# Router logits taken from residual rows that are not normalised, with the shift's part made ahead of the second attention

## The chip, the cores and the metric

The kernel runs on one core of a Trainium2 chip. The metric is the device time of one execution, in microseconds (us). A core has five engines that run their own instruction streams and meet at semaphores: TensorE (PE; its weight loads are PEld), VectorE (DVE), ScalarE (ACT), GpSimd (POOL) and SyncE (SP). SyncE here only issues transfers from the chip's memory.

## What is computed

A first block (a hybrid of two attentions) and a second block (attention over the rows and a context, then a mixture of experts with 16 experts) are applied to 256 rows of 1024 numbers. What matters here is the path from the second attention's output to the choice of rows for each expert:

```python
x = x + g_a * mix
h2 = modulate(rmsnorm(x, norm_ffn[l]), sh_f, sc_f)        # rmsnorm(...) * (1 + sc_f) + sh_f
x = x + g_f * ec_moe(h2, w_router[l], w_gate[l], w_up[l], w_down[l])
return rmsnorm(x, norm_final)

def ec_moe(h, w_router, w_gate, w_up, w_down):
    aff = jax.nn.softmax(jnp.einsum('bnd,de->bne', h, w_router, ...), axis=-1)
    vals, idx = lax.top_k(jnp.swapaxes(aff, 1, 2), cap)   # cap = 32 rows for each expert
    # each expert: gather its rows of h, silu(a) * u, down projection, scatter-add
```

All arithmetic that matters here is float32; a float32 matmul takes two passes of PE, and the profile counts each as one instruction.

## The kernel before, in words

**Tiling.** The 256 rows are two tiles `t` of 128 partitions, the 1024 columns two halves `h` of 512 or 8 chunks of 128. A name such as `ou01` or `rT10` is a group of work with a PSUM bank of its own turn: the two digits are tile and half. `DENSE` lists the groups ahead of the second attention, `TAIL` those behind it; every engine walks through the same lists in its own program. `BANK_OF` gives each group its bank; `filled` waits until PE has filled it, `leave` releases it and `kept` waits for that release.

**The tail.** Attention output `oT` is multiplied with the output weights: `first_output` makes `ou00` and `ou01` (tile 0, L1651), `tail` makes `ou10` and `ou11` (L1588). For each, DVE multiplies with the gate (L2333) and adds into the residual rows `xn`, which lie in `x_sb` (L2335), and ACT sums the squares (L770). Behind a tile's second half, `half_root` makes the mean (L1844), POOL the inverse root (L1092), and DVE scales both halves of the tile into `rn`, which lies in `rows` (L2340). PE then transposes (`rT..`, L1125), and ACT and DVE evacuate four chunks each into `uT`, with the factor `scl[:, 2, :]` and the shift `mc[:, 0, 24:32]` applied (`turned_mod`, L789 and L1859). `logits(t)` multiplies with `wr` in four column groups of the array (`lg`, L1568), DVE copies the four partial sums (L2306), `logit_sums(t)` adds them on PE (`ls`, L1576), and `softened(t)` with `soft(t)` makes the softmax. For tile 0 all this lies within the eight chunks of `ou11`: lg0 ahead of chunk 4, ls0 ahead of chunk 6. Then `afT` transposes the affinities, DVE searches the 32 largest of each expert (L2353), while PE puts `xn` into four banks (L1611, semaphore `x_added`), `slT` and `cuT` turn the choice into a one-hot matrix, `gx0` to `gx7` gather the chosen rows of `rn` and apply factor and shift, and the experts' products follow (L1717, L1763). `unread(n)` is n transposes that nobody reads; `WARM` says after which group how many of them stand.

**The stream of weights.** SyncE issues the slots of `STREAM` in order, each into a buffer that has to be free: slot OUT0's buffer is free when `ou10` is filled, OUT1's when `ou11` is. Each slot is 128 rows of 4096 numbers. The buffers in order, around the tail: `parts` (behind `ou10`), `parts` (behind `ou11`), then buffer 8 (pieces in `tz` and `lat`, 2048 numbers a row each), buffer 9 (3072 in `late_slot`, once `xn` is complete, and 1024 in `tz`, once lg1 is filled), then half of a slot into `x_sb` itself, once `x_added` is reached (L711), and then the ring again, its first half behind the first two expert products (`half_used`, L671). SyncE works in order: whatever waits in front holds back everything behind it. All expert weights together are 48 slots; 41 of them are issued from `ou11` on.

**Ahead of the second attention** PE makes, among others, qu00, qu01, xkv00 and xkv01 (L1136), while DVE applies rotations and waits.

## Time and profile before

| | |
|---|---|
| median of 3 runs | 659.83 us (658.94 to 660.0) |
| the profiled execution | 658.71 us, its span 656.9 us |
| PE busy | 588.6 us (90% of the span), mean granted clock 0.972 |
| PEld, DVE, ACT, POOL busy | 376.2, 286.7, 219.0, 41.9 us |
| transfers | 192.56 MB, mean 293 GB/s |
| chain that ended last | PE 66%, transfers 22%, DVE 5% |

The busy shares are means over stages with different limits. The page's 40 slices tell these apart: the DMA line is at 3 to 9 tenths with two holes up to slice 26, and at 9 tenths from slice 27 to the end, while the PE line falls from 9 to between 5 and 8 there. Each slice is 16.4 us, so slice 27 begins at 443 us, where the router stands.

### The profile page before, as it was taken

What the parts mean: (1) busy time and instruction counts of PE and PEld (TensorE: products, weight loads), DVE (VectorE), ACT (ScalarE), POOL (GpSimd) and SP (SyncE); (2) the same over time, 40 slices, a digit from 0 to 9 for tenths busy, and PEclk for the clock granted to TensorE, in tenths of its full rate; (3) what the DMA queues carried; (4) which work ended last, traced back from release to release, by engine and by line L of the source; (5) the groups of instructions that cost most, each with busy time, mean ns of one, the idle gap of its engine ahead of it and who ended that gap; (6) DMA issues with size and microseconds to landing.
All of it is one profiled execution on the core that took longest, in us unless ns stands there. A gap on an engine that the chain in (4) does not pass through costs nothing.

```text
span 656.9 us, 8818 instructions
## 1 busy us (share of the span) xinstructions
PE 588.6 (90%) x3513; PEld 376.2 (57%) x3513; DVE 286.7 (44%) x683; ACT 219.0 (33%) x477; POOL 41.9 (6%) x74
## 2 busy tenths in 40 slices
PE   6999999999999999999999999998989875667685
PEld 5988877778767787748755455455352421221232
DVE  3356577585658443566737867145220110010002
ACT  4345453554524423384426755121110100010002
POOL 3000000000000000110002443000000000000000
PEclk9999999999999999999999999999999887798899
DMA  8593866657697784675569003559999999999995
GB/s 355 178 392 144 347 256 232 261 215 285 257 376 278 279 343 142 245 261 199 212 256 356 29 1 129 219 186 409 402 429 430 428 426 426 428 421 432 428 418 214
DMA packets 19465, 192.56 MB, mean 293 GB/s; under 512 B 3552, under 2 KB 4960, under 8 KB 7136
## 3 DMA queue, kind: packets, MB, share of 16 engines
q1 hardware_dynamic: 15824, 188.49, 71.8%
q10 hardware_dynamic: 3312, 1.93, 1.0%
q0 software_dynamic: 288, 1.57, 0.6%
q8 instruction: 28, 0.46, 0.3%
q14 instruction: 13, 0.11, 0.1%
HBM read 190.41 MB, written 1.05 MB: 291 GB/s over the span
## 4 chain that ended last, share of the span: by engine, by line
PE 66%; DMA 22%; DVE 5%; ACT 2%; SPq 2%; issue 1%; POOL 0%; ACTq 0%; POOLq 0%; DVEq 0%
PE bank L1148 27%; DMA ring<-in_stream 21%; PE bank L1125 6%; PE bank L1136 5%; PE bank L1717 3%; PE bank L1422 3%; PE bank L1651 2%; PE bank L1187 2%; PE bank L1588 2%; PE bank L1556 2%; SPq L733 2%; PE bank L1523 2%; PE bank L1637 2%; PE bank L1479 2%; DMA vvc<-vvc 1%
## 5 line engine op out<-in xcount | busy, mean ns | idle before, releaser
L1148 PE MATMUL bank<-weight_parts,u_parts 128*128 128x512 f32 (+2 forms) x416 | 125.7, 385 | 0.7 <-DVE weight_parts L2027 0.5
L2027 DVE TENSOR_TENSOR weight_parts<-ring,weight_parts 128x1024 fp32r<-128x1024 f32 (+2 forms) x64 | 73.2, 1180 | 38.0 <-ACT weight_parts L759 36.2
L1148 PEld LDWEIGHTS bank<-weight_parts,u_parts 128*128 128x128 f32 x416 | 75.6, 188 | 18.0 <-issue 2.8
L759 ACT ACTIVATE weight_parts<-ring 128x1024 fp32r<-128x1024 f32 (+2 forms) x64 | 63.9, 1021 | 30.3 <-PE bank L1148 22.6
L1148 PE MATMUL bank<-weight_parts,x_parts 128*128 128x512 f32 (+1 forms) x128 | 48.4, 378 | 0.0
L1148 PE MATMUL bank<-u_parts,weight_parts 128*128 128x256 f32 x192 | 36.7, 288 | 0.7 <-DVE weight_parts L2027 0.6
L1092 POOL TENSOR_TENSOR small<-small 128x1 f32<-128x1 f32 (+1 forms) x14 | 8.3, 596 | 434.0 <-DVE small L2421 207.0
L823 ACT ACTIVATE sp<-sp,small 128x128 f32<-128x128 f32 (+1 forms) x48 | 21.3, 444 | 36.3 <-DVE small L1951 36.3
L1148 PEld LDWEIGHTS bank<-u_parts,weight_parts 128*128 128x128 f32 x192 | 30.5, 192 | 1.7 <-DVE weight_parts L2027 1.0
L1039 ACT ACTIVATE sp<-bank 128x512 f32<-128x512 f32 x4 | 2.4, 597 | 74.7 <-PE bank L1717 74.7
L1148 PE MATMUL bank<-x_parts,weight_parts 128*128 128x256 f32 x96 | 27.2, 283 | 0.0
L1717 PE MATMUL bank<-ring,tz 128*32 128x512 f32 x112 | 17.3, 747 | 10.8 <-DMA ring<-in_stream 10.8
L1148 PEld LDWEIGHTS bank<-weight_parts,x_parts 128*128 128x128 f32 x128 | 24.1, 188 | 4.5
L2395 DVE TENSOR_TENSOR sp<-sp,bank 128x512 f32<-128x512 f32 x4 | 2.8, 688 | 53.2 <-PE bank L1717 53.2
L2393 DVE SCALAR_TENSOR_TENSOR sp<-sp,bank 128x512 f32<-128x512 f32 x4 | 2.8, 688 | 51.2 <-ACT sp L1039 51.2
L1136 PE MATMUL bank<-ring,lat 128*128 128x512 f32 (+2 forms) x56 | 23.0, 555 | 0.4 <-ACT vvc L759 0.4
L1125 PE MATMUL bank<-ident 128*128 128x128 f32 x124 | 18.0, 291 | 4.8 <-DMA ident<-in_ident 4.8
L1125 PEld LDWEIGHTS bank<-ident 128*128 128x128 f32 x124 | 14.6, 150 | 13.4 <-issue 7.8
L1125 PE MATMUL bank<-ident,sp 128*128 128x128 f32 x152 | 21.2, 276 | 1.1 <-DVE sp L2014 0.8
L759 ACT ACTIVATE mo<-bank 128x512 f32<-128x512 f32 (+3 forms) x20 | 10.6, 541 | 33.0 <-PE bank L1148 16.6
L1125 PEld LDWEIGHTS bank<-ident,sp 128*128 128x128 f32 x152 | 17.4, 141 | 6.4 <-issue 3.3
L1008 ACT ACTIVATE tz<-bank,small 128x128 f32<-128x128 f32 x12 | 4.5, 456 | 42.5 <-PE bank L1637 42.5
(333 smaller groups left out, 1051.4 us busy)
## 6 DMA issues: line engine op xcount, KB each, us to landing
ring<-in_stream SPq DMA_DIRECT2D x41, 2048.0 KB, 8.9
parts<-in_stream SPq DMA_DIRECT2D x11, 2048.0 KB, 27.8
qk<-in_stream SPq DMA_DIRECT2D x9, 2048.0 KB, 12.2
tabs<-in_stream SPq DMA_DIRECT2D x6, 2048.0 KB, 20.4
mo<-in_stream SPq DMA_DIRECT2D x5, 2048.0 KB, 28.9
vvc<-in_stream SPq DMA_DIRECT2D x5, 2048.0 KB, 32.1
ring<-in_stream SPq DMA_DIRECT2D x5, 1024.0 KB, 31.0
tz<-in_stream SPq DMA_DIRECT2D x4, 1024.0 KB, 27.9
```

The source lines that it names most:

```text
L733: eng.dma_start(slot_columns(name, a, b), stream[n, :, a:b]).then_inc(last_in[h][i], 16)
L759: ins = act.activation(dst, src, ACT.Copy, scale=scale)
L823: ins = act.activation(k, k, ACT.Exp, bias=nm[:, u % 2, 2 * b + q:2 * b + q + 1], accum_out=sums[:, u, 2 * b + q:2 * b + q + 1])
L1125: return pe_.transpose(dst, src, ident[0:n, 0:n])
L1136: ins = pe_.matmul(o, lhs(c), rhs(c), start=(c == 0), stop=(c == chunks - 1))
L1148: ins = pe_.matmul(o, lhs(a, c, i), rhs(b, c, i), start=(c == 0 and n == 0), stop=(c == chunks - 1 and n == 2))
L1187: ins = pe_.matmul(D_(name)[:, S * i:S * i + S], w[:, c, col + P * i:col + P * i + P], u32[:, c, :], start=(c == 0), stop=(c == KC - 1))
L1422: ins = pe_.matmul(MB[32 * j:32 * j + 32, :], csil[:, c, :], w[:, k, 512 * j:512 * j + 512], start=(c == 0), stop=(c == KC - 1), tile_posi ...
L1479: pe_.matmul(SB[0][:, :], q[:, P:S], k.rearrange("p g s -> p (g s)"), start=True, stop=True)
L1523: pe_.matmul(score_bank(u)[:, :], qmT[0:QK, h, q * P:(q + 1) * P], kmT[0:QK, h, :], start=True, stop=True)\
L1717: ins = pe_.matmul(bank[b][32 * e:32 * e + 32, :], xs[:, c, e * CAP:(e + 1) * CAP], w[e][k], start=(c == 0), stop=(c == KC - 1), tile_posi ...
L2027: dve.tensor_tensor(quarter(weight_parts[:, SLOT:], name, q), quarter(slot(name), name, q), quarter(weight_parts, name, q).bitcast(F32), A ...
```

## The change

The router's logits are linear in the normalised row, so that the row's factor 1/rms can be applied behind the product. The change takes the transposes from `xn` and not from the scaled rows, multiplies the factor `scl[:, 2, :]` into `wr` once, and adds the shift's part, `wr` times shift, as a vector over the experts:

- A new group `lgb` in `DENSE`, between qu01 and xkv00: eight matmuls of one column on PE (`shift_sums`), a copy and the scaling of `wr` on DVE. ls0 gets a second matmul that spreads that column over all rows.
- `rT..` wait for the adds into `xn` only; each half is evacuated by one plain copy. rT10 moves into `ou11`, behind chunk 4; the logits of tile 1 are made half by half, the first of them ahead of rT11.
- `half_root` goes; DVE makes the mean (`half_mean`) and doesn't wait for the root there. The scaled rows `rn`, which the gather still needs, are made by ACT (`normed_rows`), those of tile 0 behind rT01, those of tile 1 behind the second exponential.
- `softened` scales the sums with the inverse root, adds the shift's vector and takes the maximum of the result; the exponential reads that result from SBUF.
- The load into `x_sb` and the gather wait for the scaled rows (`normed`, 10).
- `WARM` has other numbers of `unread` transposes: behind `ou11` 8 and not 28, behind rT11 5 and not 10, behind lg1 2, behind ls1 10 and not 8.

The diff, without the declarations of tiles and semaphores:

```diff
-WARM = {"ou11": 28, "rT11": 10, "ls1": 8, "slT": 2, "cuT": 5}
+WARM = {"ou11": 8, "rT11": 5, "ls1": 10, "slT": 2, "cuT": 5, "lg1": 2}
...
-         "xa10", "lq1", "lk0", "lk1", "qu00", "qu01", "xkv00", "xkv01", "qwT0", "qu10", "qwT1", "kwT",
+         "xa10", "lq1", "lk0", "lk1", "qu00", "qu01", "lgb", "xkv00", "xkv01", "qwT0", "qu10", "qwT1", "kwT",
...
-TAIL = ["ou00", "ou01", "ou10", "rT00", "rT01", "ou11", "rT10", "rT11", "lg1", "ls1", "afT", "slT", "cuT", "gx0", "gx1", "gx2", "gx3",
+TAIL = ["ou00", "ou01", "ou10", "rT00", "rT01", "rT10", "ou11", "rT11", "lg1", "ls1", "afT", "slT", "cuT", "gx0", "gx1", "gx2", "gx3",
...
                     eng.wait_ge(x_added, 1)
+                    eng.wait_ge(normed, 10)
                     eng.dma_start(x_sb[:, :], stream[spare, :, 0:SLOT // 2]).then_inc(third_in[2], 16)
...
-                leave(act.activation(aff[:, t, :], D_(f"ls{t}")[:, 0:E], ACT.Exp, bias=rst[:, t:t + 1],
-                                     accum_out=rst[:, 2 + t:3 + t]), f"ls{t}")
+                act.activation(aff[:, t, :], logit[:, t, :], ACT.Exp, bias=rst[:, t:t + 1],
+                               accum_out=rst[:, 2 + t:3 + t]).then_inc(exp_done, 1)
+
+            def normed_rows(t):
+                eng.wait_ge(roots, 11 + t)
+                for h in range(2):
+                    cols = slice(512 * h, 512 * h + 512)
+                    act.activation(rn[:, t, cols], xn[:, t, cols], ACT.Copy, scale=rs[:, 14 + t:15 + t]).then_inc(normed, 1)
...
-                elif name in ("rT01", "rT11"):
-                    turned_mod(name, uT, mc[:, 0, 24:32], scl[:, 2, :])
+                elif name in ("rT01", "rT10"):
+                    filled(eng, name)
+                    t, h = int(name[2]), int(name[3])
+                    copy(uT[:, 4 * h:4 * h + 4, t * P:(t + 1) * P], D_(name)[:, :].rearrange("p (c s) -> p c s", c=4), name)
+                    if name == "rT01":
+                        normed_rows(0)
                 elif name == "ls1":
                     soft(1)
+                    normed_rows(1)
...
+            def shift_sums(name):
+                kept(eng, "modT1")
+                eng.wait_ge(const_in, 16 * (len(constants) + 1))
+                begin(name)
+                for c in range(KC):
+                    a = 32 * (c % 4)
+                    ins = pe_.matmul(D_(name)[a:a + 32, 0:1], wr[:, c, :], mc[:, 0, 24 + c:25 + c], start=(c < 4),
+                                     stop=(c >= 4), tile_position=(0, a))
+                done(ins, name)
...
+            def logits(t, h):
                 name = f"lg{t}"
-                for h in range(2):
-                    kept(eng, f"rT{t}{h}")
-                begin(name)
-                for c in range(KC):
+                if (t, h) == (0, 0):
+                    eng.wait_ge(wr_scaled, 1)
+                kept(eng, f"rT{t}{h}")
+                if h == 0:
+                    begin(name)
+                for c in range(4 * h, 4 * h + 4):
                     a = 32 * (c % 4)
                     ins = pe_.matmul(D_(name)[a:a + 32, 0:P], wr[:, c, :], uT[:, c, t * P:(t + 1) * P], start=(c < 4),
                                      stop=(c >= 4), tile_position=(0, a))
-                done(ins, name)
+                if h == 1:
+                    done(ins, name)
 
             def logit_sums(t):
                 name = f"ls{t}"
                 kept(eng, f"lg{t}")
                 begin(name)
-                done(pe_.matmul(D_(name)[:, 0:E], partial[:, t, :], fold, start=True, stop=True), name)
+                ins = pe_.matmul(D_(name)[:, 0:E], partial[:, t, :], fold, start=True, stop=True)
+                if t == 0:
+                    ins = pe_.matmul(D_(name)[:, E:2 * E], shift_part.to_broadcast([P, P]), fold, start=True, stop=True)
+                done(ins, name)
+
+            def turned_rows(name):
+                t, h = int(name[2]), int(name[3])
+                eng.wait_ge(x2_ready, 2 * t + h + 1)
+                turn_tiles(name, xn[:, t, 512 * h:512 * h + 512])
...
                         if name == "ou11" and c == 4:
-                            logits(0)
+                            logits(0, 0)
+                            logits(0, 1)
+                        if name == "ou11" and c == 5:
+                            turned_rows("rT10")
                         if name == "ou11" and c == 6:
                             logit_sums(0)
                         ins = pe_.matmul(D_(name)[:, :], oT[:, c, t * P:(t + 1) * P], w[:, c, :], start=(c == 0),
                                          stop=(c == KC - 1))
                     done(ins, name)
                 elif name[:2] == "rT":
-                    t, h = int(name[2]), int(name[3])
-                    eng.wait_ge(normed, 7 + 2 * t + h)
-                    turn_tiles(name, rn[:, t, 512 * h:512 * h + 512])
+                    if name == "rT11":
+                        logits(1, 0)
+                    if name != "rT10":
+                        turned_rows(name)
                 elif name == "lg1":
-                    logits(1)
+                    logits(1, 1)
...
+                        eng.wait_ge(normed, 10)
...
-
-                eng.wait_ge(squares, n_squares)
-                dve.scalar_tensor_tensor(ss[:, k:k + 1], ss[:, k:k + 1], 1.0 / D, ss[:, k_first:k_first + 1],
-                                         ALU.mult, ALU.add).then_inc(means, 1)
-                n_mean[0] += 1
-                eng.wait_ge(roots, n_mean[0])
...
+                    elif name == "lgb":
+                        filled(eng, name)
+                        leave(dve.tensor_copy(shift_part, D_(name)[:, 0:1]), name)
+                        kept(eng, name)
+                        dve.tensor_tensor(wr, wr, bc(scl[:, 2, :], 32), ALU.mult).then_inc(wr_scaled, 1)
...
+                eng.wait_ge(squares, 14 + 2 * t)
+                dve.scalar_tensor_tensor(ss[:, 14 + t:15 + t], ss[:, 14 + t:15 + t], 1.0 / D, ss[:, t:t + 1],
+                                         ALU.mult, ALU.add).then_inc(means, 1)
+                n_mean[0] += 1
...
-                dve.tensor_reduce(rst[:, t:t + 1], D_(name)[:, 0:E], AX_X, ALU.max, negate=True).then_inc(logit_max, 1)
+                if t == 0:
+                    dve.tensor_copy(shift, D_(name)[:, E:2 * E]).then_inc(shift_ready, 1)
+                    eng.wait_ge(shift_ready, 1)
+                eng.wait_ge(roots, 11 + t)
+                leave(dve.scalar_tensor_tensor(logit[:, t, :], D_(name)[:, 0:E], rs[:, 14 + t:15 + t], shift, ALU.mult, ALU.add),
+                      name)
                 kept(eng, name)
+                dve.tensor_reduce(rst[:, t:t + 1], logit[:, t, :], AX_X, ALU.max, negate=True).then_inc(logit_max, 1)
+                eng.wait_ge(exp_done, t + 1)
                 own(dve.reciprocal(rst[:, 4 + t:5 + t], rst[:, 2 + t:3 + t]))
                 dve.tensor_scalar(aff[:, t, :], aff[:, t, :], rst[:, 4 + t:5 + t], None, ALU.mult).then_inc(aff_ready, 1)
...
-                    if h == 1:
-                        half_root(14 + t, t, 14 + 2 * t)
-                        for w in range(2):
-                            cols = slice(512 * w, 512 * w + 512)
-                            dve.tensor_scalar(rn[:, t, cols], xn[:, t, cols], rs[:, 14 + t:15 + t], None, ALU.mult)\
-                               .then_inc(normed, 1)
-                elif name in ("rT00", "rT10"):
-                    turned_mod(name, uT, mc[:, 0, 24:32], scl[:, 2, :])
+                    if name == "ou01":
+                        half_mean(0)
+                elif name in ("rT00", "rT11"):
+                    filled(eng, name)
+                    t, h = int(name[2]), int(name[3])
+                    leave(dve.tensor_copy(uT[:, 4 * h:4 * h + 4, t * P:(t + 1) * P],
+                                          D_(name)[:, :].rearrange("p (c s) -> p c s", c=4)), name)
+                    if name == "rT11":
+                        half_mean(1)
                 elif name == "lg1":
```

## Rows read from the trace of the kernel before

**Rows 1.** The page's chain that ended last, by engine

```profile
PE 66%; DMA 22%; DVE 5%; ACT 2%; SPq 2%; issue 1%; POOL 0%; ACTq 0%; POOLq 0%; DVEq 0%
```

**Rows 2.** Chain in order of time, 489 to 606: start us, us, what

```profile
561.20 42.16 DMA ring<-in_stream
```

**Rows 3.** Stretches: us; busy us of PE, PEld, DVE, ACT, POOL; PEclk; DMA share; GB/s

```profile
442.00:444.00 2.00, 2.00 (x21) 2.00 (x19) 0.85 (x2) 0.72 (x2) 0.25 (x1) 1.00 0.93 229
444.00:460.50 16.50, 14.55 (x107) 9.19 (x106) 9.12 (x28) 2.78 (x8) 0.30 (x1) 1.00 0.99 415
460.50:462.00 1.50, 1.50 (x16) 1.01 (x19) 0.41 (x1) 0.46 (x1) 0.00 (x0) 1.00 0.84 213
462.00:606.00 144.00, 109.12 (x784) 41.27 (x776) 16.05 (x30) 10.01 (x22) 0.00 (x0) 0.91 1.01 427
606.00:648.00 42.00, 31.34 (x242) 12.05 (x234) 4.12 (x8) 2.57 (x6) 0.00 (x0) 0.92 0.97 406
```

**Rows 4.** SyncE's DMA issues in order of time, from 430: start us, us, what

```profile
432.49 9.07 SPq L707 DMA_DIRECT2D parts<-in_stream  x2
441.60 0.43 SPq L699 DMA_DIRECT2D tz<-in_stream  x1
...
454.11 0.33 SPq L712 DMA_DIRECT2D x_sb<-in_stream  x1
459.53 0.33 SPq L672 DMA_DIRECT2D ring<-in_stream  x1
```

**Rows 5.** Chain in order of time ahead of 441: start us, us, what

```profile
432.46 0.87 PE bank L1125 x8
433.33 3.44 PE bank L1588 x8
436.77 0.57 PE bank L1568 x16
...
439.26 0.13 PE bank L1576 x2
```

**Rows 6.** Timeline of the router stretch: start, us, what, [idle before <-releaser]

```profile
441.31 0.69 DVE L2333 TENSOR_TENSOR rows<-bank,vvc 128x512 f32<-128x512 f32 x1 [0.79 <-PE bank L1588]
...
442.03 0.69 DVE L2335 TENSOR_TENSOR x_sb<-x_sb,rows 128x512 f32<-128x512 f32 x1
...
443.75 0.55 POOL L1092 TENSOR_TENSOR small<-small 128x1 f32<-128x1 f32 x1 [14.36 <-DVE small L1844]
...
444.88 1.09 PE L1125 MATMUL bank<-ident,rows 128*128 128x128 f32 x8 [0.62 <-DVE rows L2340]
445.57 1.36 DVE L1859 TENSOR_SCALAR tz<-bank,small 128x128 f32<-128x128 f32 x4 [0.36 <-PE bank L1125]
...
447.61 0.64 PE L1568 MATMUL bank<-tz,small 128*32 128x128 f32 x16 [0.55 <-issue]
...
449.09 0.17 DVE L2312 TENSOR_REDUCE small<-bank 128x1 f32<-128x16 f32 x1 [0.49 <-PE bank L1576]
...
450.41 3.66 PE L1611 MATMUL bank<-x_sb,ident 128*128 128x512 f32 x8
```

**Rows 7.** Timeline around qu01, 331 to 343: PE, and DVE's idle time

```profile
330.85 7.47 PE L1136 MATMUL bank<-ring,lat 128*128 128x480 f32 x20
...
343.23 0.69 DVE L2261 COPY vvc<-bank 128x512 f32<-128x512 f32 x1 [6.48 <-PE bank L1125]
```

**Rows 8.** Timeline of the same form: lg0's weight loads; ACT's first exponential

```profile
436.70 0.38 PEld L1568 LDWEIGHTS bank<-tz,small 128*32 128x32 f32 x16 [0.76 <-issue]
...
439.63 0.28 ACT L1014 ACTIVATE small<-bank,small 128x16 f32<-128x16 f32 x1 [3.57 <-DVE small L2312]
```

**Rows 9.** Stretches, as rows 3, where PE's granted clock falls

```profile
508.00:510.00 2.00, 0.00 (x0) 0.00 (x0) 0.00 (x0) 0.00 (x0) 0.00 (x0) 1.00 1.06 438
...
512.00:514.00 2.00, 2.00 (x11) 0.78 (x4) 0.58 (x1) 0.00 (x0) 0.00 (x0) 0.50 1.00 426
```

More of the change, by code:

```diff
@@ L111 @@
           "hT00": 6, "hT01": 5, "modT2": 2, "lq0": 2, "lq1": 3, "lk0": 2, "lk1": 3, "afT": 0, "slT": 1,
-          "rT00": 2, "rT01": 3, "rT10": 4, "rT11": 5, "lg0": 6, "ls0": 7, "hT10": 2, "hT11": 3, "kc0": 4, "kc1": 5, "qm0": 4, "qm1": 5, "kx0": 6, "kx1": 7, "lg1": 6, "ls1": 7, "cuT": 7,
+          "rT00": 2, "rT01": 3, "rT10": 4, "rT11": 5, "lgb": 4, "lg0": 6, "ls0": 7, "hT10": 2, "hT11": 3, "kc0": 4, "kc1": 5, "qm0": 4, "qm1": 5, "kx0": 6, "kx1": 7, "lg1": 6, "ls1": 7, "cuT": 7,
           **{f"gx{c}": (2, 7, 1)[c % 3] for c in range(KC)}}
@@ L427, in build @@
         rst = tiny(8)
+        logit = tiny(2 * E).rearrange("p (t e) -> p t e", t=TOK)
+        shift = tiny(E)
+        shift_part = tiny(1)
         affT = view(pt, 1024, 256)
@@ L527, in build @@
         aff_ready = sem("aff_ready")
+        exp_done = sem("exp_done")
+        wr_scaled = sem("wr_scaled")
+        shift_ready = sem("shift_ready")
         top_found = sem("top_found")
@@ L1194, in unread @@
                     turn(o[:, 0:P], ident[:, :])
+            def shift_sums(name):
[7 more added lines that the diff above has]
+                done(ins, name)
             def dense(name):
-                if name[:2] == "xT":
+                if name == "lgb":
+                    shift_sums(name)
+                elif name[:2] == "xT":
                     t, h = int(name[2]), int(name[3])
@@ L1559, in pair_pv @@
                     ins.then_inc(u_pv, 1)
-            def logits(t):
+            def logits(t, h):
                 name = f"lg{t}"
-                for h in range(2):
-                    kept(eng, f"rT{t}{h}")
-                begin(name)
-                for c in range(KC):
+                if (t, h) == (0, 0):
[4 more added lines that the diff above has]
+                for c in range(4 * h, 4 * h + 4):
                     a = 32 * (c % 4)
```

2 lines of the change are left out of this document (1 added, 1 removed).

## The prediction

> **What bounds the kernel now.** I read the page's chain first, then the chain and the transfers in the stretch that the change touches, then the engines. By the page's chain PE holds 66% of the span and the transfers of `stream` 22% [rows 1]; the chain in order of time says which holds which part: from 490.07 on three long links are waits for a transfer, the longest of 42.16 us, with short PE links between them [rows 2]. The table of stretches says why: from 462 to 606 us the transfers run at 427 GB/s with a DMA share of 1.01, from 606 to 648 at 406 [rows 3]. So behind about 442 us the end is set by bytes: the expert weights that are still to come, at a fixed rate, from the moment the queue last had room to waste. The lost places in that stretch are few: the queue is empty before 442, it moves 229 GB/s from 442 to 444, and 213 GB/s from 460.5 to 462 [rows 3].
>
> SyncE's issues tell what ends each idle time. The transfer into `parts` for slot OUT1 is the second of the pair at 432.49; that entry lasts 9.07 us, so the second goes out at about 441.2, when group `ou11` is filled. `tz` follows at 441.60, `lat` and `late_slot` right behind, then the rest of `tz`, `x_sb` at 454.11, and nothing more before the ring's first half at 459.53, which waits for the first expert products [rows 4]. By their shapes in the code (128 rows of 4096, 2048, 2048, 3072, 1024 and 2048 numbers of 4 bytes) that is 2.10 + 1.05 + 1.05 + 1.57 + 0.52 + 1.05 = 7.34 MB from 442 on; the table gives 0.229 x 2 + 0.415 x 16.5 = 7.3 MB up to 460.5 [rows 3]. So the queue runs dry at 460.5, about 1 us after the ring's issue, and the 213 GB/s is what a queue does that has just been filled again.
>
> Ahead of 442 the chain is PE: transposes of rT00 and rT01 0.87 us, the first half of `ou11` 3.44, lg0 0.57, two more of its chunks, ls0 0.13 and the last two, with no wait between them [rows 5]. The router proper, from the last add into `xn` (442.03 + 0.70) to the reduction at 449.09, lies beside the transfers already queued [rows 6].
>
> **The change part by part.** Every size is in us of the profiled execution (658.71, span 656.9).
>
> 1. The shift's column, `lgb`, is 8 two-pass matmuls of one column on PE between qu01 and xkv00. PE there works 7.47 us on end [rows 7], so it is all on the path; nothing between there and `ou11` is timed by a transfer, and whatever waits on DVE or ACT is itself fed by PE, so the delay goes through to 441 us. No row has a matmul of one column. Bounds: from 0.2 (half of 0.38) to 1.0 (the 0.57 of lg0, 16 passes of 128 columns [rows 5], and 0.43 beside it, a pass of `ou11` by 3.44 / 8 [rows 5], for leaving and entering the split of the array). A gain is excluded, since nothing is removed there. The 16 weight loads of 32 columns of lg0 took 0.38 busy [rows 8], and one column leaves nothing else: I take **+0.4**. The copy and the scaling of `wr` on DVE (about 0.2 and 0.4, below the 0.69 of an operation of 512 columns) fall into the 6.48 us in which DVE waits for PE [rows 7]: nothing; without that cover 0.6.
>
> 2. Ahead of `ou11`'s end, the transposes of rT10 go in (half of the 0.87 for eight, **+0.44**) and a second matmul in ls0 (**+0.13**, the price of the present one) [rows 5]. Splitting lg0 in two adds no instruction. Does PE wait there? rT00 and rT01 now need only the adds of `xn`, done earlier than the normalised rows. ACT has one copy of 512 columns and two scaled copies in place of four small ones (some 0.7 each, by the 0.69 of DVE's add over 512 columns [rows 6]) and then rT10's copy; it sat idle 3.57 us before 439.63 [rows 8], so it is ready before PE delivers rT10 at about 438.7. DVE's four small scalings of 1.36 us [rows 6] become one copy of about 0.7. In `softened(0)` DVE gets a copy, a scale-and-add and a wait on a larger chain, some 0.5 more ahead of the add behind `ou11`; DVE waited 0.79 us there [rows 6]. So no new stall: the issue of `parts` behind `ou11` comes 0.4 + 0.57 = **0.97 later**, bounds 0.6 and 1.6.
>
> 3. The router behind `ou11`. Now: add ends 442.73, square on ACT, mean, POOL's root 0.55 from 443.75, rows scaled, transposes from 444.88, halves evacuated in 1.36 on DVE beside ACT, logits at 447.61, sums, reduction from 449.09 [rows 6]. After: transposes of rT11 alone at 442.76, DVE's copy from 443.45 (0.69 after the transposes start, as 445.57 stands to 444.88) to 444.14, four matmuls, partial at 444.63 (half of 0.64 and the latency), 0.29, sums at 444.96, 0.43 to the scale-and-add at 445.39, 0.24, reduction from 445.67. The square, mean and root run beside it: the mean now queues behind DVE's copy (444.14), so the root is there by 444.3 + 0.07 + 0.55 = 444.9, before 445.39. That is 3.4 us sooner than 449.09; less the 0.57 of part 2, the search, `x_added`, gather and first products come **2.9 sooner** (less 0.4 for `lgb`). The new scaled rows on ACT (some 0.7 each behind the second exponential, so by about 447.7) are ready long before the gather, which comes behind the search, and before the load into `x_sb`, which gets a new wait for them on SyncE's queue; behind that load stands the whole expert stream, but its other wait, `x_added`, ends at about 451, so the new one costs nothing (it would cost from 451 on).
>
> 4. What of that reaches the end? Only what keeps the queue from running dry. The ring's half goes out at 459.53 - 2.9 = 456.6, the queue now drains at 460.5 + 0.57 = 461.1 (both moved alike by `lgb`), so 4.4 us of transfers stand behind it and the thin stretch goes: (427 - 213) / 427 x 1.5 = 0.75, **-0.75**. Bounds 0 (the thin stretch stays) and 1.0 (with the 229 GB/s of the first 2 us: 0.93 lost at another restart). Later releases had room enough already: the rate is 427 throughout.
>
> Here the Trainium skill makes it a little larger: "DMA: Bandwidth & Descriptors", section Anatomy of one DMA, gives a transfer (on GpSimd's path) about 2.0 us of fixed cost beside its bytes. By that page, as an estimate, a transfer issued 0.97 us before the queue is empty shows 1.03 us of it, and the sum would be 0.28 lower than by the row; the trace's 0.75 decides.
>
> **Sum**: 0.4 + 0.57 - 0.75 = +0.2. Against the profiled 658.71 that is 658.9; the median of the runs stands 1.12 above that execution at 659.83, so 660.0. Three runs of before spread from 658.94 to 660.0; a difference under about 0.2% (1.3 us) is what a measurement of this kernel cannot tell from none.
>
> **The rivals.**
> A, the router's time reaches the end: were the kernel waiting for the router, 2.9 less 0.4 would come off, 657.3. For it: the router is the only PE-idle stretch near 445. Against it: 427 GB/s from 462 on [rows 3], and waits of PE for transfers in the chain [rows 2]. The delayed `parts` issue alone forbids it.
> B, the costs stay and the gain doesn't: the ring's half goes out earlier but a thin stretch remains, as it follows every refill (229 GB/s at 442) [rows 3]. Then +0.97, 660.8; with `lgb` at its upper bound 1.0, 661.4, which is past 0.2%.
> C, slower by PE's clock. The change cuts the idle-fillers behind `ou11` from 28 to 8 and behind rT11 from 10 to 5, and PE has gaps there. The rows show the clock go from 1.00 to 0.50 (2.4 to 1.2 GHz) behind 508 to 510, in which PE did nothing, and stay low up to 514 [rows 9]. At 1.2 GHz from 444 on, `x_added`'s eight products take 7.3 for 3.66 [rows 6], and the gather and first products behind them, of about that length, some 3 more: the ring's half at 456.6 + 3.7 + 3 = 463.3, 2 us behind the drained queue. With the 0.97 that is +3.0, 662.8. It decides once the low clock eats more than the 4.4 us of part 4. Against it: with 8, 5, 2 and 10 fillers no gap I work out above exceeds 0.6 us, and the fall in the rows came behind 2 us without any product.
> The Trainium skill speaks against the change here: "TensorE: Matmul & The Clock Gate", section What's actually happening, says that the throttled state is the default and that activity releases it. By that page fewer fillers risk what C describes; this trace has 1.00 from 442 to 462 with the fillers in [rows 3], and no row with them out.
>
> **How the numbers follow.** Forecast (net between -0.4 and +1.2, B's plain case in it): 0.80. A, or a like gain: 0.06. C: 0.06. B with a dear `lgb` or a stall inside `ou11` that I don't see: 0.08. Hence faster 0.06, same 0.80, slower 0.14. Range: the forecast's -0.4 (0.6 - 1.0) on 659.83, less the 0.9 by which the fastest run of before lies under its median, gives 658.5; up to B's upper end 661.4. C and A stay outside.
>
> **What the profile of the changed kernel would show.** Part 1: 8 matmuls of one column near 335 us and the window scores later by 0.4. Part 2: the second `parts` issue at about 442.1, `ou11`'s last add ending at about 443.7. Part 3: `x_added`'s first product at about 447.9 (was 450.41), the ring's half issued at about 457.0. Part 4: above 400 GB/s throughout from 446 to 606, and the last transfer landing at 648.3. I am wrong if the rate between 446 and 462 still has a hole, if PEclk is below 1.00 before 500, or if PE waits inside `ou11`.

## The result, and the profile after

| | before | after |
|---|---|---|
| median | 659.63 us (16 runs, 658.79 to 660.83) | 660.82 us (16 runs, 659.7 to 661.89) |
| the profiled execution, its span | 658.71, 656.9 | 660.60, 658.8 |
| ratio | | 1.0019, 95% interval 1.0013 to 1.0026 |

The change costs 1.2 us, 0.19%. The forecast was 660.0, a change within 0.2%, in a range of 658.5 to 661.4: the direction holds, and the time is 0.8 above the forecast. That 0.8 is the interesting part, because nearly every step ahead of it came out as written.

The chain that ended last, in order of time (start us, us, what), around qu01 and then ahead of 443, where [rows 7] and [rows 5] stood:

```profile
331.40 3.87 PE bank L1154 x12
335.28 0.24 PE bank L1220 x16
335.51 3.65 PE bank L1154 x8
...
433.30 0.87 PE bank L1143 x8
434.17 3.44 PE bank L1632 x8
437.61 0.58 PE bank L1600 x16
438.18 1.05 PE bank L1632 x2
439.24 0.44 PE bank L1143 x4
439.67 0.86 PE bank L1632 x2
440.53 0.13 PE bank L1609 x2
440.66 0.22 PE bank L1611 x2
440.89 1.83 PE bank L1632 x4
```

L1220 is `lgb`: 0.24, and with the slower re-entry into L1154 the stretch is 0.44 longer than in before (7.76 for 7.32). Inside `ou11` stand rT10's 0.44 and the shift's product, 0.13 and 0.22. There is no wait between the links.

SyncE's issues (start us, us, what) and the timeline of the router, where [rows 4] and [rows 6] stood:

```profile
433.33 9.73 SPq L713 DMA_DIRECT2D parts<-in_stream  x2
443.10 0.43 SPq L705 DMA_DIRECT2D tz<-in_stream  x1
...
452.30 0.33 SPq L719 DMA_DIRECT2D x_sb<-in_stream  x1
457.74 0.33 SPq L678 DMA_DIRECT2D ring<-in_stream  x1
```

```profile
443.53 0.69 DVE L2392 TENSOR_TENSOR x_sb<-x_sb,rows 128x512 f32<-128x512 f32 x1
444.28 0.66 PE L1143 MATMUL bank<-ident,x_sb 128*128 128x128 f32 x4 [0.35 <-DVE x_sb L2392]
444.97 0.69 DVE L2398 COPY tz<-bank 128x512 f32<-128x512 f32 x1 [0.75 <-PE bank L1143]
445.72 0.42 PE L1600 MATMUL bank<-tz,small 128*32 128x128 f32 x8 [0.24 <-DVE tz L2398]
446.99 0.23 DVE L2366 SCALAR_TENSOR_TENSOR small<-bank,small 128x16 f32<-128x16 f32 x1 [0.49 <-PE bank L1609]
447.26 0.17 DVE L2369 TENSOR_REDUCE small<-small 128x1 f32<-128x16 f32 x1
448.61 3.66 PE L1656 MATMUL bank<-x_sb,ident 128*128 128x512 f32 x8
```

`tz` goes out 1.50 later than in [rows 4] and the ring's half 1.79 sooner. From the last add's start to the reduction it is 3.73 us, where [rows 6] have 7.06.

The stretches (us; busy us of PE, PEld, DVE, ACT, POOL; PEclk; DMA share; GB/s), against [rows 3]:

```profile
442.00:444.00 2.00, 1.93 (x18) 1.09 (x16) 1.62 (x5) 0.01 (x1) 0.00 (x0) 1.00 0.57 115
460.50:462.00 1.50, 1.50 (x17) 0.66 (x10) 0.00 (x0) 0.00 (x0) 0.00 (x0) 1.00 0.99 410
462.00:606.00 144.00, 105.43 (x762) 39.87 (x764) 16.06 (x30) 10.03 (x22) 0.00 (x0) 0.92 1.01 427
```

The 213 GB/s of 460.5 to 462 have become 410. Adding up the GB/s of stretches of 1 us from 440 on gives the time of each megabyte: the changed kernel is 1.65 behind at the seventh (461.32 for 459.67) and 0.74 at the eighth (463.71 for 462.97), and 0.67 at the eightieth (632.35 for 631.68). So the gain of 0.75 to 0.9 came, where it was forecast. Of the 0.67, 0.40 was there at 330 us already, ahead of everything that is changed (the `parts` issue at 329.89 for 329.49); this is chance of one execution, since the twelve profiles of the experiments, of kernels like either, have it between 329.74 and 330.32. By bytes the change costs 0.27, and 0.2 was forecast.

But the last transfer landed 1.88 later, not 0.67. That landing sets the end: from it to the end of the span it is 8.80 us in both traces. The chain's last wait for one (start us, us), of before and of after:

```profile
619.88 28.23 DMA ring<-in_stream
```

```profile
620.95 29.04 DMA ring<-in_stream
```

And the last stretches of the stream, columns as above, of before:

```profile
646.00:647.00 1.00, 1.00 (x16) 0.52 (x12) 0.00 (x0) 0.00 (x0) 0.00 (x0) 1.00 0.57 233
647.00:648.00 1.00, 0.55 (x8) 0.07 (x8) 0.38 (x1) 0.00 (x0) 0.00 (x0) 1.00 0.06 25
```

of after:

```profile
646.00:647.00 1.00, 0.00 (x0) 0.00 (x0) 0.20 (x1) 0.00 (x0) 0.00 (x0) 1.00 0.72 274
647.00:648.00 1.00, 0.45 (x8) 0.29 (x12) 0.00 (x0) 0.00 (x0) 0.00 (x0) 1.00 0.40 164
648.00:649.00 1.00, 1.00 (x16) 0.55 (x8) 0.00 (x0) 0.00 (x0) 0.00 (x0) 1.00 0.07 29
649.00:650.00 1.00, 0.78 (x10) 0.16 (x8) 0.15 (x1) 0.00 (x0) 0.00 (x0) 1.00 0.03 12
```

The core's transfers are shared by 16 DMA engines, and 427 GB/s over 16 is 27 each. For 1.4 us, from 648.1 on, the changed kernel's transfer is one engine finishing alone, with a DMA share of 0.07, one sixteenth. Its table of transfers from 648 to 650, in 40 slices of 0.05 us, shows the packets one by one (82 GB/s for 0.05 us is 4 KB):

```profile
GB/s 0 0 164 0 0 0 82 0 0 82 0 0 82 0 0 82 0 0 82 0 0 82 0 0 82 0 0 82 0 0 0 0 0 0 0 0 0 0 0 0
```

### The profile page after: what moved, and what is told of

Its sections match the earlier page's. It is cut to its first block, busy times and chain, and to the rows that moved or that the text cites. A ratio compares the mean times of both kernels' runs of the same rounds, so it can differ in the third digit from the quotient of the medians.

```text
span 658.8 us, 8809 instructions
## 1 busy us (share of the span) xinstructions
PE 588.9 (89%) x3510; PEld 374.0 (57%) x3510; DVE 284.8 (43%) x678; ACT 219.9 (33%) x475; POOL 42.0 (6%) x74
## 4 chain that ended last, share of the span: by engine, by line
PE 65%; DMA 23%; DVE 5%; ACT 2%; SPq 2%; issue 1%; POOL 0%; ACTq 0%; POOLq 0%; DVEq 0%
PE bank L1166 26%; DMA ring<-in_stream 21%; PE bank L1143 6%; PE bank L1154 5%; PE bank L1763 4%; PE bank L1452 3%; PE bank L1697 2%; PE bank L1205 2%; PE bank L1632 2%; PE bank L1586 2%; SPq L740 2%; PE bank L1553 2%; PE bank L1683 2%; PE bank L1509 2%; DMA vvc<-vvc 1%
## 5 line engine op out<-in xcount | busy, mean ns | idle before, releaser
L1763 PE MATMUL bank<-ring,tz 128*32 128x512 f32 x112 | 18.9, 807 | 11.4 <-DMA ring<-in_stream 11.4
L1154 PE MATMUL bank<-ring,lat 128*128 128x512 f32 (+2 forms) x56 | 23.2, 556 | 0.4 <-ACT vvc L766 0.4
L1763 PE MATMUL bank<-parts,tz 128*32 128x512 f32 x112 | 14.6, 651 | 6.6 <-DMA parts<-in_stream 6.6
L1143 PE MATMUL bank<-ident 128*128 128x128 f32 x103 | 15.8, 294 | 4.7 <-DMA ident<-in_ident 4.7
L1143 PEld LDWEIGHTS bank<-ident 128*128 128x128 f32 x103 | 12.2, 150 | 13.5 <-issue 8.0
```

The lines of the kernel that those rows point to most:

```text
L1143: return pe_.transpose(dst, src, ident[0:n, 0:n])
L1154: ins = pe_.matmul(o, lhs(c), rhs(c), start=(c == 0), stop=(c == chunks - 1))
L1763: ins = pe_.matmul(bank[b][32 * e:32 * e + 32, :], xs[:, c, e * CAP:(e + 1) * CAP], w[e][k], start=(c == 0), stop=(c == KC - 1), tile_posi ...
```

## What the late engine is: a theory and its rival

Every slot is spread over all 16 engines, and the trace records 16 landings of it, one for each engine's part. In the steady part the last lies 1.9 (before) and 2.25 us (after) behind the first. In the changed kernel, nine times from 460 on, one engine's landings fall back by 1.5 to 1.7 us against the others and stay there; each time a packet of the page's queue q8, "instruction", 16 KB, has gone out 2 to 6 us earlier (a slot takes 4.9), and there are nine such packets in that stretch. Two of them lie where this case is decided, the one at 460 and the last at 645. The lines of q8 (packets, MB, share) in the changed kernel's table of transfers, from 458.5 to 463.5 and from 644.5 to 646:

```profile
q8 instruction: 1, 0.02, 1.2%
...
q8 instruction: 1, 0.02, 4.4%
```

The second is 4.4% of 16 engines for 1.5 us, or 1.06 us of one engine. Before has them at 459.1 and 643.8. The Trainium skill, "Runtime: NRT & Kernel Launch", section Instruction fetch mechanics, says that each engine's sequencer fetches its own instructions in blocks of 16 KB by DMA, at a cost that is mostly hidden; the packets' size agrees, while the cost shows here on a DMA engine that the weights need, by the 1.5 to 1.7 us above. The rows don't name an engine; e11 below shows that they are PE's.

**Theory 1**: the end follows the bytes, as the prediction had it; the tail is another thing that the change brought. **Theory 2**: the end is set by the slowest of 16 engines. A thin stretch costs each engine time, but an engine that is behind makes up for its delay there. The thin stretch of before stood right behind the fetch of 459.1 and took up part of its 1.55: the engine hit there lands 1.67 behind the first in the slot under way, and 0.94 behind it in the next. (Another engine fell back to 1.86 in the thin stretch itself and stayed there.) Without the thin stretch the bytes gain 0.8, the engine hit near 460 keeps its delay (1.83 and 1.82 in the changed kernel's two slots), and the last fetch puts it further behind. The offsets of the 16 landings of the last slot of the stream, in us from the first of them, taken from the trace:

```
before          0 .10 .24 .28 .39 .82 .85 1.45 1.52 1.53 1.61 1.66 1.72 1.72 1.81 2.21
after           0 .05 .07 .18 .45 .74 .79 1.07 1.46 1.48 1.66 1.74 1.75 1.95 2.24 3.45
e9_before_early 0 .03 .07 .24 .48 .75 .79 1.51 1.58 1.60 1.62 1.62 1.63 1.65 1.88 3.23
e11_few_fillers 0 .10 .18 .34 .51 .59 .99 1.08 1.55 1.61 1.64 1.67 1.75 1.81 1.82 1.83
```

In before the engine that falls back last was 0.8 behind the first and ends at 2.21; in after it was 1.9 behind and ends at 3.45. Followed from slot to slot, these are the offsets of the engines that were hit near 460. A jump of this kind at the last fetch is seen in e1, e2, e4 and e6 to e9 as well: the last of the 16 lies 1.9 to 2.2 behind the first until the last fetch, and 3.0 to 3.7 from then on. I call the last number of such a row the spread.

## The experiments

The experiments were measured in three groups (e1 to e4, e5 to e8, e9 to e12), each beside its own runs of the kernel before (medians 659.60, 659.28 and 659.56). "By bytes" is the time of the 80th megabyte less the time of the `parts` issue near 330, against the mean of two profiles of before (302.19 and 302.23); this takes out what one execution had lost by then. The spread of before is 2.21 and 2.46, mean 2.33.

| kernel | median less before's | by bytes | spread, less 2.33 | sum of the two |
|---|---|---|---|---|
| the change | +1.19 | +0.25 | 3.45, +1.12 | +1.4 |
| e6 the same again | +1.41 | -0.3 | 3.68, +1.35 | +1.1 |
| e1 16 transposes in `ou11` | +2.25 | +2.0 | 2.98, +0.65 | +2.6 |
| e2 router 1.6 later | +0.98 | +0.2 | 3.04, +0.7 | +0.9 |
| e3 router 6.4 later | +3.78 | +3.6 | 1.69, -0.65 | +2.9 |
| e4 tile 0's router behind `ou11` | -0.39 | -2.6 | 3.19, +0.85 | -1.7 |
| e7 `lgb` in idle time | +1.37 | -0.3 | 3.48, +1.15 | +0.9 |
| e8 rT10 behind `ou11` | +0.69 | -0.5 | 3.23, +0.9 | +0.4 |
| e9 before, router shorter | +0.26 | -0.9 | 3.23, +0.9 | 0.0 |
| e10 router 4.3 later | +2.30 | +1.4 | 3.29, +0.95 | +2.3 |
| e11 few fillers | -0.18 | -0.1 | 1.83, -0.5 | -0.6 |
| e12 all that gains | -3.23 | -2.4 | 2.13, -0.2 | -2.6 |

The medians come from up to 16 runs, bytes and spread from one execution, which lies up to 1.2 beside its median (e4). So the fair comparison is with the time of that same execution, less its `parts` issue near 330 and less the same for before (329.31 in the mean): there the sum is right within 0.5 us in every row but e7's (1.4 for the change, 0.0 for e9, -1.5 for e4, -2.8 for e12). In e7 the time is 2.0 for a sum of 0.9, because PE was still busy when the last transfer had landed: from there to the end of the span it is 9.9 us, and 8.8 in the other thirteen traces. Against the medians the sum is up to 1.3 off (e4) and mostly low. The bytes alone fit neither: the medians of the change itself, e4 and e6 to e9 are 0.9 to 2.2 above them.

**e1, the issue behind `ou11`.** 16 more unread transposes ahead of `ou11`'s last chunk:

```diff
+                        if name == "ou11" and c == 7:
+                            unread(16, bank[3])
```

> The changed kernel with 16 unread transposes put ahead of the last chunk of ou11 on PE (0.11 us each by the fillers' row, 1.8 us together); nothing else. Theory 'queue' (behind ou11 the end is set by the bytes from the issue of OUT1's buffer on): the second parts issue comes 1.8 us later and the whole kernel is 1.8 us longer than the changed one, so about 3.0 us over the kernel before. Rival 'router' (the time is set by the router's chain, of which ou11 is a part as well): also about 1.8, but then e2 has to cost its 2.2 too; the pair tells them apart. Rival 'cover' (PE's time ahead of ou11 is hidden by the transfers): under 0.5.

Measured: 661.85, ratio 1.0028 (1.0013 to 1.0043); `tz` goes out at 444.70, 1.60 later than in the changed kernel, and the bytes run 1.6 to 1.7 later with it. Time ahead of `ou11`'s end is paid in bytes one for one. The median rose by only 1.1 over the change's (2.25 less 1.19), where 1.8 was expected; the spread here was 2.98 and not 3.45.

**e2, e3, the router's own time.** Idle-filling transposes ahead of tile 1's softmax, 30 and 70 for 10:

```diff
-WARM = {"ou11": 8, "rT11": 5, "ls1": 10, "slT": 2, "cuT": 5, "lg1": 2}
+WARM = {"ou11": 8, "rT11": 5, "ls1": 30, "slT": 2, "cuT": 5, "lg1": 2}
```

> The changed kernel with 20 more unread transposes behind ls1 (30 for 10), which lie ahead of afT: the search, x_added, the gather and the ring's first half come up to 2.2 us later. Part of the fillers hides in PE's wait for the affinities, where 10 stand already. Theory 'queue': the ring's half is issued at up to 459.9 and not 457.7, the queue has transfers until about 462, so the time stays that of the changed kernel within 0.5 us; a thinner stretch of the rate may come back (at most 0.75). Rival 'router': 2 us longer than the changed kernel, some 3.2 over the kernel before.

> As e2, with 60 more fillers behind ls1 (6.6 us). Theory 'queue': the ring's half is issued at about 464.0, 2 us after the queue has run dry at about 462; the lost 2 us and a restart of 1 us show, so 3 us longer than the changed kernel, and the transfers show a hole of 2 us at 462. Rival 'router': 6.3 us longer.

Measured: e2 660.58, ratio 1.0014 (0.9998 to 1.0031), with the ring's half at 459.32, 1.6 later; e3 663.38, 1.0058 (1.0036 to 1.0080), with it at 464.11, 6.4 later. So the router has 1.6 us to spare at least, and a delay of 6.4 reaches the bytes with 3.3 to 3.6: rival A is refuted, and the picture of part 4 stands. In e3 the last wait for a transfer ended only 2.03 later than in the changed kernel though its bytes were 3.3 to 3.6 later; this was the first sign that an empty queue takes something off the tail.

**e4, e8, what stands inside `ou11`.** e8 moves rT10's transposes behind `ou11`. e4 moves all of tile 0's router and leaves out 13 of the unread transposes (the diff, without the order of the steps on PE, ACT and DVE that goes with it):

```diff
-TAIL = ["ou00", "ou01", "ou10", "rT00", "rT01", "rT10", "ou11", "rT11", "lg1", "ls1", "afT", "slT", "cuT", ...
+TAIL = ["ou00", "ou01", "ou10", "ou11", "rT00", "rT01", "rT10", "rT11", "lg1", "ls1", "afT", "slT", "cuT", ...
-WARM = {"ou11": 8, "rT11": 5, "ls1": 10, "slT": 2, "cuT": 5, "lg1": 2}
+WARM = {"ls1": 10, "slT": 2, "cuT": 5, "lg1": 2}
```

> The changed kernel with all of tile 0's router work (transposes of rT00 and rT01, lg0, ls0 with the shift's product) and rT10 moved on PE from ahead of ou11's end to behind it; DVE and ACT are reordered to suit, and the softmax of tile 0 stands beside that of tile 1. On PE 0.87 + 0.58 + 0.44 + 0.13 + 0.22 = 2.2 us go from ahead of ou11's end. Theory 'queue': the second parts issue comes 2.2 us earlier than in the changed kernel and the time falls by 2.2 us (1.0 us below the kernel before), though the affinities are only about 1.2 us earlier; the ring's half comes at 456.5, the queue drains at 459.8. Rival 'router': it falls by the 1.2 us by which the affinities are earlier. Rival 'cover': no change.

> The changed kernel with the four transposes of rT10 moved on PE from within ou11 to right behind it, and ACT's copy of them behind the first exponential. Theory 'queue': 0.44 us go from ahead of ou11's end, the second parts issue comes 0.44 earlier against the first, the affinities at most 0.5 later against it, the ring's half still ahead of the drained queue: 0.4 us less than the changed kernel. Rival 'router': no gain, or a loss, since the router's chain gets no shorter.

Measured: e4 659.21, ratio 0.9987 (0.9972 to 1.0003), `tz` at 440.79, 2.31 sooner than in the changed kernel, bytes 2.6 to 2.7 sooner; e8 659.97, 1.0016 (1.0006 to 1.0027), from `parts` to `tz` 9.33 us where the changed kernel has 9.77. With the router not on the path that sets the end, each product inside `ou11` costs its price, and behind it nothing. e4's median is 1.6 under the change's (from +1.19 to -0.39), where 2.2 was expected, and its profiled execution 2.6 (span 656.2 for 658.8); its bytes gained 2.8. Its stream, too, ends with one engine at 3.19.

**e7, `lgb`.** The shift's column between lk0 and lk1, where PE waits:

```diff
+                if name == "lk1":
+                    shift_sums("lgb")
                 if name == "lgb":
-                    shift_sums(name)
+                    pass
```

> The changed kernel with the eight one-column products of lgb put on PE between lk0 and lk1, where PE waited 0.59 us for DVE; DVE's part stays behind qu01. Theory 'queue': lgb's price of 0.24 (its own link in the chain) to 0.44 (the shift from 331 to 350) goes, every later issue up to ou11 comes 0.25 to 0.45 earlier, and so does the end: ratio to the changed kernel 0.9995. Rival: the 0.44 was something else, and the parts issue at 433 stays where it is against that at 330 (103.44 us apart).

Measured: 660.65, ratio 1.0025 (1.0013 to 1.0036), beside e6's 660.69. From the `parts` issue near 330 to that near 433 it is 103.02 us, with the changed kernel 103.44 and with before 103.00: `lgb` costs 0.42 there and the edit gives it back. The time shows nothing of it; 0.4 us is less than this comparison can tell, so that the gain of this edit in time is not shown.

**e5, e6, both kernels again**, beside e7 and e8.

> The kernel before, unchanged, for a second profile. In the first pair of profiles the changed kernel stood 0.40 us later already at 329.9 us (the parts issues), ahead of any edit, and the last piece of the stream landed 1.88 us later although the bytes moved lay only 0.7 later. If both are chance of one execution, this profile has the parts issues anywhere between 329.5 and 330.1 and the wait for the last piece ends anywhere between 648 and 650. If they belong to the kernels, it repeats 329.5 and 648.1 within 0.2.

> The changed kernel, unchanged, for a second profile and a ratio taken beside the other kernels. Chance of one execution: the parts issues between 329.5 and 330.2, the last wait ends between 648.8 and 650.2. If they belong to the kernel: 329.9 and 650.0. The ratio should repeat 1.0019 within 0.0008.

Measured: before, one execution, 659.60; the change 660.69, ratio 1.0022 (1.0013 to 1.0030). Their last waits for a transfer end at 648.99 and 650.53 and their spreads are 2.46 and 3.68, so the tail is no accident of the first pair.

**e9, the thin stretch alone.** The kernel before, with its ring's half sooner. It leaves out tile 1's own factor (tile 1 is scaled with tile 0's root) and two of the four rounds of the search:

```diff
-                        half_root(14 + t, t, 14 + 2 * t)
+                        if t == 0:
+                            half_root(14, 0, 14)
+                        else:
+                            eng.wait_ge(x2_ready, 4)
...
-                            dve.tensor_scalar(rn[:, t, cols], xn[:, t, cols], rs[:, 14 + t:15 + t], None, ALU.mult)\
+                            dve.tensor_scalar(rn[:, t, cols], xn[:, t, cols], rs[:, 14:15], None, ALU.mult)\
...
                     turned_mod(name, uT, mc[:, 0, 24:32], scl[:, 2, :])
+                    if name == "rT10":
+                        half_root(15, 1, 16)
...
-                    for i in range(CAP // 8):
+                    for i in range(2):
```

> The kernel before, with its router shortened: tile 1's rows are scaled with tile 0's root, so that nothing waits for the sum of squares, and the search makes 2 of its 4 rounds (both leave part of the router out). Nothing ahead of ou11's end changes, so tz goes out at about 441.6 (plus the execution's own drift), and the ring's half about 2 us sooner, near 457.6, ahead of the empty queue. Theory 1 (the gain of the missing thin stretch reaches the end): no stretch under 300 GB/s at 460 to 462, and the time falls by 0.75 to 0.9 under before, to about 658.8. Theory 2 (it refills the 16 DMA engines but not the one that ends last, which a code fetch delays twice, near 460 and near 645, each by 1.55): the bytes run 0.7 to 0.9 ahead of before from 463 to 643, but the last wait for a transfer ends within 0.3 of where it ended in before, and the time is 659.4 to 659.8, as before.

Measured: 659.82, ratio 1.0002 (0.9993 to 1.0011). The ring's half went out at 458.92 with `parts` 0.30 later at 330, so it came 0.9 sooner by the program, less than the 2 I expected, and that was enough. The stretches, of e9:

```profile
460.50:462.00 1.50, 1.50 (x15) 0.54 (x18) 0.31 (x1) 0.46 (x1) 0.00 (x0) 1.00 1.03 426
...
646.00:647.00 1.00, 0.93 (x16) 0.42 (x16) 0.00 (x0) 0.00 (x0) 0.00 (x0) 1.00 0.28 115
647.00:648.00 1.00, 1.00 (x16) 0.58 (x12) 0.00 (x0) 0.00 (x0) 0.00 (x0) 1.00 0.06 25
```

426 for 213 GB/s, the 80th megabyte at 631.13 for 631.68 in spite of those 0.30, and the last wait for a transfer ends at 648.52 for 648.11, 0.1 later without them. This is the cleanest of the runs: it changes the thin stretch, and neither `ou11` nor the number of PE's instructions. The thin stretch went, the bytes gained 0.85, and the time gained nothing: the interval, -0.5 to +0.7 us, leaves out -0.75. The engine that had been hit at 458.9 kept its delay (1.81, later 1.75) and was hit again by the last fetch, to 3.25. The step that the prediction put at -0.75 is worth 0 in this kernel.

**e10, a thin stretch put back.** `"ls1": 50` for 10 in the changed kernel.

> The changed kernel with 40 more idle-filling transposes ahead of tile 1's softmax (50 for 10): the ring's half goes out about 3.9 us later than in the changed kernel, near 461.8, just as the queue is empty, so that a short thin stretch comes back. Theory 1 (the end follows the bytes): the bytes are about 1.2 later than in the changed kernel and the time is 1.2 higher, 662.0. Theory 2 (a thin stretch lets the engine that a code fetch had delayed catch up): the bytes are about 1.2 later as well, but the last landing is no more than 0.4 later, time 660.8 to 661.2.

Measured: 661.86, ratio 1.0037 (1.0024 to 1.0049), theory 1's number. The ring's half went out at 462.07 and two thin stretches followed (the same columns):

```profile
462.00:463.50 1.50, 1.50 (x15) 0.71 (x7) 0.00 (x0) 0.00 (x0) 0.00 (x0) 1.00 0.71 224
463.50:465.00 1.50, 1.50 (x17) 0.68 (x19) 0.41 (x1) 0.46 (x1) 0.00 (x0) 1.00 0.85 295
```

Theory 2's number was missed: the spread stayed at 3.29. The 40 transposes are 80 more instructions, and they moved the fetches as well, that of 460.5 to 453.0, 9 us ahead of the thin stretch, and the last to 642.3. In before the thin stretch began 1.4 us behind the fetch. Nor does the spread come from the last fetch here: a fetch at 488.7 hit an engine that was 1.85 behind, and that engine is 3.4 behind from then to the end, while the last fetch hit one at 1.3 and brought it to 2.9. So this run changed two things, and what a thin stretch gives back stays bounded only by before against e9 and by e3, whose spread was 1.69.

**e11, the last fetch moved.** 30 of the 32 transposes left out of the changed kernel:

```diff
-WARM = {"ou11": 8, "rT11": 5, "ls1": 10, "slT": 2, "cuT": 5, "lg1": 2}
+WARM = {"ls1": 2}
```

> The changed kernel with 30 of its 32 idle-filling transposes left out (2 stay, behind ls1). They cost PE instructions and no wait, so the ring's half stays near 457.7 if PEclk stays 1.00, and the bytes stay as in the changed kernel up to 643. The last code fetch of PE, at 645 in the changed kernel, comes some 60 instructions later in the program, about 8 to 10 us, behind the last transfer. Theory 1 (the tail's 1.2 us have another cause than the fetch): time as the changed kernel, 660.7. Theory 2 (the last fetch delays the engine that is behind already): the last wait for a transfer ends 1.0 to 1.5 sooner, time about 659.5. If PE's granted clock falls to 0.50 behind ou11 (rival C of the prediction), the ring's half comes at 463 and later, and the time is 661 to 663.

Measured: 659.38, ratio 0.9998 (0.9988 to 1.0008): 1.3 us under the changed kernel by removing work that no one waits for. The bytes are those of the changed kernel (632.44 for 632.35, with `parts` at 330 0.43 later). The last packet of q8 went out at 648.2 and not 645.1, behind what the engine that it met still had to bring, and the others moved back with it, that of 563.7 to 574.0. Only PE's program is shorter, so the packets of q8 are PE's instructions. The spread is 1.83. In the changed kernel it was 2.26 ahead of the last fetch and 3.45 behind it, so that 1.2 of the difference are the last fetch and 0.4 lie further ahead. The end of the stream (columns as above), where the changed kernel has 164, 29 and 12:

```profile
647.00:648.00 1.00, 1.00 (x16) 0.51 (x12) 0.00 (x0) 0.00 (x0) 0.00 (x0) 1.00 0.58 238
648.00:649.00 1.00, 0.75 (x12) 0.22 (x16) 0.39 (x1) 0.00 (x0) 0.00 (x0) 1.00 0.11 33
649.00:650.00 1.00, 1.00 (x11) 0.32 (x3) 0.46 (x2) 0.00 (x0) 0.00 (x0) 1.00 0.00 0
```

e11 also shows rival C's mechanism, PE's granted clock without the fillers:

```profile
444.00:448.00 4.00, 1.91 (x16) 1.01 (x16) 2.13 (x6) 0.80 (x3) 0.55 (x1) 0.92 0.98 332
448.00:452.00 4.00, 3.15 (x6) 1.52 (x7) 2.75 (x11) 1.55 (x4) 0.00 (x0) 0.50 0.97 410
452.00:456.00 4.00, 3.86 (x11) 1.59 (x9) 1.33 (x5) 0.00 (x0) 0.00 (x0) 0.72 1.04 438
```

PE worked 1.91 of 4 us from 444 on, then ran at 0.50 (1.2 GHz) for 4 us and longer, and the ring's half went out at 460.63, 2.9 us later. The queue still had transfers, so that this cost nothing.

**e12, all that gains.** e4's order, e7's place for `lgb`, e11's `WARM`.

> All that gained or might gain at once: tile 0's router moved whole behind ou11 (nothing but ou11's own chunks ahead of its end), the shift's column made between lk0 and lk1, and 30 of the 32 idle-filling transposes left out. Theory 1 (the end follows the bytes; fetches don't matter): the bytes run 2.5 ahead of the changed kernel, time about 658.8. Theory 2 (the last fetch also falls behind the stream): another 1.2 less, about 657.6, ratio to before 0.997. If PE's clock falls with so few transposes, the ring's half comes behind the empty queue and the time is 660 or more.

Measured: 656.33, ratio 0.9950 (0.9937 to 0.9962), 3.2 us under the kernel before and 1.3 under the 657.6 expected. `tz` went out at 440.16, the ring's half at 457.45, the spread is 2.13, and the last wait for a transfer is 27.77 us long and ends at 645.80. The last fetch, at 644.9, came 0.5 us ahead of the end of the stream's last packet and moved none of the 16 landings. Where the 1.3 beyond theory 2's number come from is open; the profiled execution itself is 2.8 faster than before's by the count of the table, for a sum of 2.6. The three edits were not taken apart here.

## Why the prediction was right, and where it was not

The direction came out and the time lies in the range, the second partly by luck: the costs were priced well, one gain was priced at 0.75 and was worth nothing, and the range held that case only because rival B had put it there for another reason.

1. **`lgb` +0.4**: right; 0.42 to 0.44 in the chain and by e7. Copy and scaling on DVE (0.16 and 0.43) lay in idle time.
2. **0.97 later behind `ou11`**: the change's own part came out at 1.10 (`tz` 1.50 later, less 0.40 of the execution). Of the 0.13 too little, 0.09 is the second product of ls0, 0.22 and not 0.13. No stall inside `ou11`; DVE's idle time ahead of L2390 shrank from 0.79 to 0.28. (The lower bound of this part, 0.6, does not follow from the prediction's own numbers: 0.2 for `lgb` and 0.57 make 0.77. The range's lower end would be 0.2 higher by it, and the result is far from that end.)
3. **Router 2.9 sooner**: the ring's half came 1.79 sooner, 2.2 without the execution's 0.40, where the forecast's 2.9 less 0.4 says 2.5. From the add's end to the reduction it was 3.04 us (444.22 to 447.26) for 6.36 in before, so 3.3 sooner where 3.4 was worked out; the rest is the 0.13 of point 2. The mean ran at 445.58 behind DVE's copy, and POOL's root was there at 446.4, ahead of the scale-and-add at 446.99. The 0.3 cost nothing, as e2 shows.
4. **The thin stretch, -0.75**: the step that failed. The rate was as forecast (410 for 213 GB/s), and so was the gain in bytes (1.65 - 0.74 = 0.9). Its place in the sum was wrong: I took it that what all 16 engines gain together the end gains. e9 shows the same gain in bytes with no gain in time (+0.26, interval -0.5 to +0.7). With 0 in its place the prediction's own sum is 0.97, 660.8, and 660.82 was measured. That is rival B's number, but not by its reason: B said that the thin stretch would stay, and it went.

The term itself was worth 0 because the end of the stream is set not by the queue as a whole but by the last of its engines (the tail's landings, 3.45 apart for 2.21). A transfer counts as landed when the last of its 16 parts has; the Trainium skill says the same in "DMA: Bandwidth & Descriptors", section Why a DMA increments its semaphore by 16 and not by 1. A row of GB/s is a sum over engines and can't show it; the tail's rows, with a DMA share of 0.07, can. In the profile of before this was to be read: 25 GB/s from 647 to 648.

By the fixed cost of 2.0 us in the Trainium skill, "DMA: Bandwidth & Descriptors", section Anatomy of one DMA, the sum would have been 0.28 lower still; the bytes gained 0.9, between its 1.03 and the row's 0.75, and the time gained none of it. PE's clock, last: with 2 fillers for 32 the clock fell to 0.50 (e11), with the change's 32 it stayed at 1.00 from 440 to 460. The rule of the Trainium skill's "TensorE: Matmul & The Clock Gate", section What's actually happening, that the throttled state is the default, agrees with this. Rival C therefore names a real mechanism whose price the prediction overestimated: 2.9 us of router were taken up by the queue, since at half clock the ring's half came at 460.6 and not 463.3.

What stays open: that the fetches of 460 and 645 met the same engine in after is read from the offsets of the landings (1.83 behind the first at 462, 1.87 at 641, 3.47 at 644, with the nearest other engines at 1.78 and 1.98) and fits e9 and e11, but the trace gives no engine's name, and why these two fetches meet one engine isn't shown; and how much a thin stretch gives back as a function of its distance from the fetch (e10) wasn't settled.

## What to carry to other kernels

Where a stream of transfers sets the end, look at its last 3 us before pricing anything by GB/s: if they run at one sixteenth of the rate, the end belongs to one engine, and what only the other fifteen gain is worth nothing. Instructions that no one waits for are not free there: they bring fetches of 16 KB, each of which holds one engine up by 1.5 us. Here 60 fewer of them moved the last fetch behind the stream, and that was worth 1.3 us. And work that is off the path is best moved behind the point that frees the next buffer, even if this makes its own chain longer: e4's order alone brought the bytes 2.6 us forward.

## What the runs showed of the hardware that was not expected

- A 16 KB packet of q8 takes 0.9 to 1.1 us of one DMA engine and puts this engine 1.5 to 1.7 us back against the other fifteen. In before, at 459.1, the rest is the 8 KB packet right behind it on the same engine, which took 0.81 us for the usual 0.31. With the queue full the engine did not catch up in any of these traces; the offsets lasted from slot to slot until an engine was hit again.
- The smaller packets of the other instruction queue, q14 (8 KB), do the same on a smaller scale: in before one at 635.0 put an engine back by 0.7.
- The place of the last fetch in the stream was worth 1.3 us (e11 against the change), with 60 instructions.
- Sixteen passes of one column took 0.24 in the chain, 0.31 in the timeline, and 0.44 with the way back into full matmuls, against 0.57 to 0.58 for sixteen of 128 columns. Two passes of 16 columns from a broadcast operand took 0.22, where the two before them took 0.13.
